# Seven block products in half of one output projection: forgetting attention in a two-block transformer kernel on one Trainium2 core

## What is computed

```python
h = x @ w_in                      # q, k, v, forget logits, gate: 4 x 1024 + 16 columns
cum = jnp.cumsum(log_sigmoid(f_logit + b_f), axis=1)
o = _dense_causal(q, k, v, 64 ** -0.5, cum)          # 16 heads of 64
y = (o * jax.nn.silu(gate)) @ w_out                  # w_out: 1024 x 1024
x = _layernorm(8 ** 0.25 * x + y, ln_g, ln_b)
```

## Time and profile before

| | |
|---|---|
| median of three runs | 1783.54 us (1783.27 to 1784.11) |
| the profiled execution | 1783.37 us |
| its span, first to last instruction | 1781.6 us |
| PE busy | 1762.7 us, 99% of the span |
| DVE, ACT, POOL busy | 992.2, 811.2, 727.9 us |
| share of PE in the chain that ended last | 89% |
| mean granted TensorE clock | 0.998 of full |

### The profile page before, as it was taken

How to read it: one execution, slowest core, us unless ns; L and a number is a source line. 1 busy time by engine, 2 the same in 40 slices (tenths; PEclk the granted TensorE clock), 3 DMA queues, 4 the chain that set the end, 5 groups by cost and what they waited for, 6 DMA issues and landing times.

```text
span 1781.6 us, 24874 instructions
## 1 busy us (share of the span) xinstructions
PE 1762.7 (99%) x9776; PEld 1416.7 (80%) x9776; DVE 992.2 (56%) x2091; ACT 811.2 (46%) x1737; POOL 727.9 (41%) x441
## 2 busy tenths in 40 slices
PE   9999999999999999999999999999999999999997
PEld 6787877788888888889776798888877777887676
DVE  4558688564351524254777368755644352567764
ACT  5434455453342323244467345554345343446662
POOL 4534521154686868643322333234332324332122
PEclk9999999999999999999999999999999999999999
DMA  5322320153505151333212232123331322331211
GB/s 173 100 71 72 95 60 25 36 174 93 170 25 177 36 165 48 95 90 93 60 36 83 83 99 72 60 71 94 97 92 50 79 63 90 99 68 38 63 52 72
DMA packets 215032, 147.94 MB, mean 83 GB/s; under 512 B 51825, under 2 KB 197249, under 8 KB 214914
## 3 DMA queue, kind: packets, MB, share of 16 engines
q1 hardware_dynamic: 210592, 137.10, 26.6%
q10 hardware_dynamic: 4322, 9.24, 1.6%
HBM read 144.22 MB, written 2.10 MB: 82 GB/s over the span
## 4 chain that ended last, share of the span: by engine, by line
PE 89%; DVE 7%; ACT 3%; issue 1%; DMA 0%; POOL 0%; SPq 0%; DVEq 0%; ACTq 0%
PE PS L427 24%; PE PS L429 23%; PE PS L428 23%; PE PS L515 6%; PE PS L577 6%; PE PS L601 4%; PE PS L779 1%; DVE PS L1645 1%; ACT X L1172 1%; DVE X L1648 1%; DVE PS L1664 1%; PE PS L1033 1%; PE PS L802 1%; PE PS L1054 0%; DVE P L2188 0%
## 5 line engine op out<-in xcount | busy, mean ns | idle before, releaser
L2291 POOL TENSOR_TENSOR Wl<-Wr,Wh 128x1024 fp32r<-128x1024 f32 (+3 forms) x367 | 601.6, 1660 | 1001.9 <-ACT Wh L1113 1001.6
L427 PE MATMUL PS<-XTl,Wh 128*128 128x512 f32 (+1 forms) x1096 | 412.9, 377 | 1.0 <-DVE KF L1683 0.8
L429 PE MATMUL PS<-XTh,Wh 128*128 128x512 f32 (+1 forms) x1096 | 408.1, 372 | 0.0
L428 PE MATMUL PS<-XTh,Wl 128*128 128x512 f32 (+1 forms) x1096 | 408.0, 372 | 0.0
L1113 ACT CAST Wh<-Wr 128x1024 fp32r<-128x1024 f32 (+5 forms) x274 | 249.3, 931 | 154.5 <-PE PS L429 96.1
L427 PEld LDWEIGHTS PS<-XTl,Wh 128*128 128x128 f32 x1096 | 206.5, 188 | 45.6 <-issue 9.9
L429 PEld LDWEIGHTS PS<-XTh,Wh 128*128 128x128 f32 x1096 | 206.4, 188 | 36.5
L428 PEld LDWEIGHTS PS<-XTh,Wl 128*128 128x128 f32 x1096 | 206.6, 188 | 34.7
L427 PE MATMUL PS<-Wl,XTh 128*128 128x512 f32 (+2 forms) x608 | 227.3, 374 | 1.7 <-DVE XTl L1656 1.2
L429 PE MATMUL PS<-Wh,XTh 128*128 128x512 f32 (+2 forms) x608 | 224.1, 369 | 0.0
L428 PE MATMUL PS<-Wh,XTl 128*128 128x512 f32 (+2 forms) x608 | 224.0, 368 | 0.0
(11 more groups left out here) (342 smaller groups left out, 2748.7 us busy)
## 6 DMA issues: line engine op xcount, KB each, us to landing
Wr<-in_w_in SPq DMA_DIRECT2D x38, 512.0 KB, 3.6
Wr<-in_fox_w_in SPq DMA_DIRECT2D x32, 512.0 KB, 4.2
Wr<-in_w_ffn_gate SPq DMA_DIRECT2D x22, 512.0 KB, 3.9
Wr<-in_w_ffn_up SPq DMA_DIRECT2D x22, 512.0 KB, 3.9
Wr<-in_swa_w_in SPq DMA_DIRECT2D x20, 512.0 KB, 3.8
WP<-in_w_ffn_down SPq DMA_DIRECT2D x9, 1024.0 KB, 9.2
Wr<-in_mla_w_in SPq DMA_DIRECT2D x16, 512.0 KB, 4.1
Wr<-in_mla_w_out SPq DMA_DIRECT2D x16, 512.0 KB, 3.2
```

What stands on the lines that cost most here:

```text
L427: pe.matmul(o, l[0], r[1], start=start, stop=False, skip_group_check=again)
L428: pe.matmul(o, l[1], r[0], start=False, stop=False, skip_group_check=again)
L429: return pe.matmul(o, l[0], r[0], start=False, stop=stop, skip_group_check=again)
L2291: ins = raw.tensor_tensor(l[:, cs], r[:, cs], h[:, cs].bitcast(F), sub)
```

## The change

In `fox`, the contraction tiles a = 0..3 of the output projection are computed by Winograd's form of the product of 2x2 blocks, with seven block products instead of eight; a = 4..7 stay as they were. Tile pairs (0,1) and (2,3) are q = 0 and q = 1. For each q the left factor becomes seven 256-token factors, the weights four raw pieces: the even row with its right half replaced by a sum ("even"), two sums of halves ("sums"), the odd row as it is ("odd"), and one more sum ("fours", of which both q share one piece). Gate 3 and gate 5 get a new step `factors` on ACT and DVE; `gated` is left out for f = 0..3; POOL gets `sums7`; the odd rows are loaded twice, once for the sums and once as a piece. PE runs `outproj7`; DVE folds four partial results per token half into `X` (`combine`) before the residual. The due number at the last gate projection (`g7`) is one higher. PE's part and the pieces:

```diff
+SEVENS = {'fox': (3, 5)}
...
+            if c in SEVENS and kind in ("sums", "fours"):
+                return O7[c][1 if kind == "sums" else 2][:, :, :].rearrange("p a n -> p (a n)")
...
+        def released(entry):
+            if entry in odd_of:
+                return by_pool.at("fours", *homes[odd_of[entry]][1:])
+            return weight_lo.at(entry)
...
+        def overlaid(s, q):
+            if s == "fox":
+                return [scores_full.at(s, 3 + 3 * q, 1, 3)]
...
-                    due[signal, key] = min(count[0] + AHEAD + (key[:2] == ("swa", 1)) + 2 * (key == ("fu", 21)), len(used) + W_SLOTS)
+                    due[signal, key] = min(count[0] + AHEAD + (key[:2] == ("swa", 1)) + 2 * (key == ("fu", 21)) + (key == ("g", "fox", 7)), len(used) + W_SLOTS)
...
+            def outproj7(s, src, lhs, ready, turned=True):
+                A, B, C, E = ([take(("y", s, v + i, c)) for v in range(2)] for i, c in ((0, 0), (2, 1), (0, 1), (2, 0)))
...
+                def product(bs, v, w, h, j, q, start, stop, again=False):
+                    e.wait_ge(weight_lo.at(w), *free(bs[v]), by_dve.at("fs", s, q))
+                    return mm3(PS[bs[v]][:, :], [t[:, q, j, tile(v)] for t in FS], part(w, 0, D, 512 * h, 512 * h + 512), start, stop, again)
+                for q in range(2):
+                    w2 = weight(row(2 * q), D, ("even", s, q))
+                    odd_src[w2] = row(2 * q + 1)
+                    w13 = weight(row(2 * q), D, ("sums", s, q))
+                    for bs, w, h, j, x in ((A, w2, 0, 0, "A"), (B, w2, 1, 5, "B"), (C, w13, 0, 4, "C"), (E, w13, 1, 3, "E")):
+                        for v in range(2):
+                            ins = product(bs, v, w, h, j, q, q == 0, q == 1)
...
+                for q in range(2):
+                    wo = weight(row(2 * q + 1), D, ("odd", s, q))
+                    if q == 0:
+                        w4 = weight(row(0), D, ("fours", s, 0))
+                    for bs, w, h, j, x in ((A, wo, 0, 1, "A"), (C, wo, 1, 6, "C"), (E, w4, q, 2, "E")):
+                        for v in range(2):
+                            e.wait_ge(by_dve.at("part", s, x, v))
+                            ins = product(bs, v, w, h, j, q, False, False, again=True)
...
+                ws = [(weight(row(a), D), a) for a in range(4, 8)]
+                for i in range(NT):
+                    for c in range(2):
+                        b, fresh = place[i, c], i >= 2 and c == 1
```

ScalarE's part of `factors`, and the call in its list of steps:

```diff
+            def factors(s, q):
+                g = GT[s][:, 2 * q:2 * q + 2, :].rearrange("p f (a t) -> p (f a) t", a=2)
+                e.wait_ge(by_dve.at(s, "o", 2 * q + 1), *overlaid(s, q))
+                high(FS[0][:, q, 0, :], g[:, 0, :], "fs_hi", s, q)
+                high(FS[0][:, q, 1:3, :], g[:, 2:4, :], "fs_hi", s, q)
+                e.wait_ge(by_dve.at("sf", s, q))
+                high(FS[0][:, q, 3:7, :], S4[:, :, :], "fs_hi", s, q)
...
-                elif kind == "out":
+                elif kind == "gate" and x in SEVENS.get(s, ()):
+                    factors(s, SEVENS[s].index(x))
+                elif kind == "out" and (x >= 4 or s not in SEVENS):
                     gated(s, x)
```

VectorE's `combine` and its part of `factors`:

```diff
+            def combine(s):
+                for x in "ACEB":
+                    for v in range(2):
...
+                        e.wait_ge(psum_full.at("part", s, x, v), by_dve.now())
+                        if x in "AB":
+                            scale = ALPHA if x == "A" else 1.0
+                            ve.scalar_tensor_tensor(low, low, scale, b, mult, add).then_inc(*by_dve.next())
+                            ve.scalar_tensor_tensor(right, right, scale, b.unsqueeze(1).broadcast_to([128, 2, 512]), mult, sub).then_inc(*by_dve.next("part", s, x, v))
+                        else:
+                            y = X[:, v + 2, HALVES[1]]
+                            ve.tensor_tensor(y, y, b, add if x == "C" else sub).then_inc(*by_dve.next("part", s, x, v))
...
+            def factors(s, q):
+                ve.tensor_tensor(S4[:, 0, :], g[:, 0, :], g[:, 1, :], sub).then_inc(*by_dve.next())
+                ve.tensor_tensor(S4[:, 1, :], g[:, 1, :], g[:, 3, :], sub).then_inc(*by_dve.next())
+                e.wait_ge(by_dve.now())
+                ve.tensor_tensor(S4[:, 2, :], S4[:, 1, :], g[:, 0, :], sub).then_inc(*by_dve.next())
+                e.wait_ge(by_dve.now())
+                ve.tensor_tensor(S4[:, 3, :], S4[:, 2, :], g[:, 2, :], add).then_inc(*by_dve.next("sf", s, q))
+                e.wait_ge(by_act.at("fs_hi", s, q), by_dve.now())
+                low(FS[1][:, q, 0, :], g[:, 0, :], FS[0][:, q, 0, :], "fs", s, q)
+                low(FS[1][:, q, 1:3, :], g[:, 2:4, :], FS[0][:, q, 1:3, :], "fs", s, q)
+                low(FS[1][:, q, 3:7, :], S4[:, :, :], FS[0][:, q, 3:7, :], "fs", s, q)
```

GpSimd's sums, called before the rest of the piece "even" of q, and SyncE's loop:

```diff
+            def sums7(i, s, q):
+                e.wait_ge(raw_in[slots[0]].at(i), raw_in[slots[1]].at("odd", i), *([weight_lo.at(at_home["sums", s, 0])] if q else [by_dve.at("fs", s, 1)] if s == "swa" else []))
+                raw.tensor_tensor(t[:, 0, :], w[:, HALVES[0]], w[:, HALVES[1]], add).then_inc(*by_pool.next())
+                raw.tensor_tensor(t[:, 1, :], w[:, HALVES[1]], o[:, HALVES[1]], add).then_inc(*by_pool.next("sums", s, q))
+                e.wait_ge(by_pool.now())
+                raw.tensor_tensor(w[:, HALVES[1]], t[:, 0, :], o[:, HALVES[1]], add).then_inc(*by_pool.next("even", s, q))
+                e.wait_ge(by_pool.now())
+                raw.tensor_tensor(f[:, q, :], w[:, HALVES[1]], o[:, HALVES[0]], add).then_inc(*by_pool.next("fours", s, q))
...
+                for key, srcs in ((i, srcs), (("odd", i), odd_src.get(i))):
...
+                    if ring[key] >= RAW_SLOTS:
+                        e.wait_ge(released(ringed[ring[key] - RAW_SLOTS]))
```

More of the change, by code:

```diff
@@ L560, in outproj, with row @@
                     if norm and turned and i in (1, 2):
+                        turn_tile(s, i - 1)
+                used[ws[-1][0]] = psum_full.at("y", s, NT - 1, 1)
+            def outproj7(s, src, lhs, ready, turned=True):
+                A, B, C, E = ([take(("y", s, v + i, c)) for v in range(2)] for i, c in ((0, 0), (2, 1), (0, 1), (2, 0)))
+                place = {(v + i, c): bs[v] for bs, i, c in ((A, 0, 0), (B, 2, 1), (C, 0, 1), (E, 2, 0)) for v in range(2)}
+                FS = O7[s][0]
+                def row(a):
+                    return [(src[:, a:a + 1, :], 0)]
+                def product(bs, v, w, h, j, q, start, stop, again=False):
[8 more added lines that the diff above has]
+                            ins = product(bs, v, w, h, j, q, q == 0, q == 1)
+                            if q:
+                                ins.then_inc(*done(psum_full, "part", s, x, v))
+                        if h:
+                            if not q:
+                                ins.then_inc(*weight_used.next())
+                            used[w] = psum_full.now() if q else weight_used.now()
+                for q in range(2):
[6 more added lines that the diff above has]
+                            ins = product(bs, v, w, h, j, q, False, False, again=True)
+                        if h:
+                            ins.then_inc(*weight_used.next())
+                            used[w] = weight_used.now()
+                ws = [(weight(row(a), D), a) for a in range(4, 8)]
+                for i in range(NT):
+                    for c in range(2):
+                        b, fresh = place[i, c], i >= 2 and c == 1
+                        if fresh:
+                            e.wait_ge(by_dve.at("part", s, "B", i - 2))
+                        for w, a in ws:
+                            e.wait_ge(weight_lo.at(w), *ready(a))
+                            ins = mm3(PS[b][:, :], pair(lhs, ALL, a, tile(i)), part(w, 0, D, 512 * c, 512 * c + 512), fresh and a == 4, a == 7, again=not fresh)
+                            if i == NT - 1 and c == 1 and a < 7:
+                                ins.then_inc(*weight_used.next())
+                                used[w] = weight_used.now()
+                        ins.then_inc(*done(psum_full, "y", s, i, c))
+                        give(b, (by_dve, ("normed", s, i, c)))
+                    if turned and i in (1, 2):
@@ L1091, in tensor @@
                     give(b, (by_dve, (s, "o", x)))
-            outproj(s, by_rows(A["fox_w_out_2"][0]), XT, lambda a: [by_dve.at("fox", "out", a)])
+            outproj7(s, by_rows(A["fox_w_out_2"][0]), XT, lambda a: [by_dve.at("fox", "out", a)])
             mla(1)
@@ L2119, in mla @@
                         gate_values(s, x)
-                    elif kind == "out":
+                        if x in SEVENS.get(s, ()):
+                            factors(s, SEVENS[s].index(x))
+                    elif kind == "out" and (x >= 4 or s not in SEVENS):
                         gated(s, x)
```

70 lines of the change are left out of this document (53 added, 17 removed).

## The result

The changed kernel takes 1788.08 us (median of 12 executions, 1785.72 to 1790.33) against 1783.77 us (12, 1782.65 to 1784.22) of the kernel before: 1.0024 times as long, 95% interval 1.0015 to 1.0032. The forecast was 1785.8 in a range that ended at 1787.6.

What follows compares the result with a forecast made beforehand. PE was taken to bound the kernel, busy 1762.7 of 1781.6 us. It would lose 2.72 us of matmuls but wait for late pieces, reaching a = 7 2.3 us later: 1783.54 + 2.3 = 1785.8, range 1783.0 to 1787.6.

Steps and rivals of the forecast that it cites:

- Slower clock: Rival, 13%: PE stands twice around 1508 to 1512, the granted clock falls to its lower level, adding 1.8 us; 1787.6.
- The copies: DVE's `PT` copies of pair 6 wait behind the second half's factors at gate 5 and come 5.0 us late.
- The scaling: ACT's scaling of pair 7, behind the late DVE work, goes from 1469.69 to 1474.7, 5.0 us late.
- The tanh: ACT's tanh of g7, behind rounding of POOL's late sums, starts at 1485.9 instead of 1483.63, 2.3 us late.
- Gate 7: On DVE, behind rests of f = 4 to 6 beside POOL's, gate 7 starts at 1491.7, 2.6 us late.
- POOL's row: POOL's seven weight-piece rests in a row begin 3.77 us after gate 7, at 1495.45 instead of 1492.85.
- The first half's factors: The factors made at gate 3 cost nothing: 5 us on DVE inside 8.42 idle us.
- Turns: DVE's and POOL's rests alternate an instruction at a time near gate 7; without turns, a 15% rival, 1783.4.
- PE's 2.72 us: In the projection's half a = 0..3, PE does 84 matmuls instead of 96, which takes 2.72 us from it.
- The sum: PE gets to a = 7 of part (0,0) at 1512.05 instead of 1509.76, so the kernel is 2.3 us slower.
- PE's stands on the way: PE waits about 1.7 us at the first round's last bank, 1.5 at a = 6 and 1.7 at a = 7.
- Where the 2.72 went: The account of the saved PE time as lost in three PE waits: last bank, a = 6 and a = 7.

Runs made afterwards that it cites:

- e1: The changed kernel run again with no edit, for its spread and a second profile: 1788.11 us, 1.0025 times the kernel before.
- e4: The changed kernel with six useless matmuls ahead of a = 6 and six ahead of a = 7 in part (0,0): 1785.40 us.
- e5: The changed kernel without the higher due number for the last gate, so ACT rounds three pieces ahead of it and not four: 1789.25 us.
- e6: The changed kernel with POOL's two rests that run beside DVE's rests 4 to 6 cut into four instructions each: 1785.84 us.
- e9: The changed kernel with second-half factors at gate 4, ACT rounding one piece ahead of them, and the second round reordered to free the "fours" slot earlier: 1781.59 us.
- e2: The changed kernel with the second half's factors at gate 4 instead of gate 5: 1784.07 us, 1.0006 times the kernel before.
- e3: The changed kernel with gate 7 ahead of DVE's rests of f = 4 to 6 in `fox`: 1784.93 us, 1.0009 times the kernel before.

## Why the prediction was wrong

The step that failed is a term of the sum: it put the clock behind PE's stands at nothing. The prediction had the schedule, its stands and the price of the clock, "Slower clock, 1787.6 (+4.1)", and gave that rival 13% against 64% for the same schedule at full clock. The runs turn it round: nine of the change's twelve executions have the lower mean clock, and all seven of e1; with the stands filled (e4) none has. The rival's price was about right: 1.8 forecast from the program's first matmuls, 1.80 measured between the two stages, 1.6 of it by the clock. What spoke for it was in the trace and was read as nothing: "there is no row of so broken a stretch at full speed" was a reason not to expect full speed. Nor was the stand of 1.33 at 1099.30 read. It has the full clock behind it in the trace before and the lower level in e5 and e6, so that row alone would have misled. The range ended exactly on the rival's value, 1787.6, and left its own scatter out; the median lies 0.48 above. Of this 0.23 belongs to the kernel before, which had 1783.77 beside the change and not 1783.54.

Point by point for the rest:

- The copies 5.0 us late: 4.99. The scaling 5.0: 5.00. The tanh 2.3: 2.39. Gate 7 2.6: 2.58. POOL's row 2.6 (1492.85 to 1495.45): 2.58. The first half's factors and `combine`: no wait of PE on either in the change's projection; before the first residual DVE still sits idle for 8.05.
- Turns: right for the rests, as e6 shows. f = 4 to 6 were to be done 4.6 us after 1487.15; the three took 4.50.
- PE's 2.72 us: right. The 84 matmuls of the sevens run from 1486.04 to 1504.98 in e9, 18.94 us from the first start to the last, and the first 84 before take the same (1485.83 to 1504.77). What e9 lacks of the 2.72 is the 0.32 at a = 7.
- The sum: a = 7 of part (0,0) starts 2.27 later than before, and +2.29 was reckoned (1512.05 for 1509.76). This is the chain through POOL's row, step by step, and no luck. PE's stands on the way were less exact. They were to be 1.7, 1.5 and 1.7, counted by PE's starts; by its starts they are 1.17 (1490.35 to 1491.74, less the usual 0.23), 1.49 and 1.54. The brackets in the timeline (1.00, 1.33, 1.37) are shorter, since they begin when the matmul ahead has ended. And PE came to the projection 0.50 late, put at "a few tenths". Neither moves a = 7, which waits for POOL.
- A stand costs more than its bracket: from the first to the last of the 84 matmuls the change takes 1485.69 to 1505.96, 1.33 us longer than e9, with a bracket of 1.00 in it.
- "Where the 2.72 went" left out a bound: even with the row in time, a = 7 waits for the slot of "fours" (1.59 in e2 and e3). It did not show in the change, but undoing the late factors alone would not have brought the gain.

Open: what decides, behind the same stands, whether the clock falls in an execution.

## What to carry to other kernels

A change that leaves PE less work and another engine no less turns a full PE into one that stands now and then; price each such stand twice, by its wait and by the clock behind it, and where no row shows the engine standing like this at full clock, give the slower case at least an even chance. When an edit's gain is eaten by waits, look for the next wait in line too: taking away the late factors alone (e2) brought the seven products back to the old time, and only with the slot of "fours" freed as well did they pay. Put side work on an engine into the stretch where it idles, and check which instruction of a neighbour it will have to take turns with.

## What the runs showed of the chip that was not expected

- Behind stands of 1.01, 1.30 and 1.56 us the clock was at its lower level for most of four windows of 1 us (0.53, 0.50, 0.50, 0.77 in e1); behind 1.00, 1.33 and 1.37 in the same program it stayed at 1.00 (the change's first profile). A single stand of 1.32 at about 1100 us was followed by the lower level in two profiles (e5, e6) and by the full clock in eight.
- Twelve useless matmuls made the kernel 2.7 us faster (e4 against e1), 1.74 of it in the stage.
- Cutting POOL's rests in four cost POOL 1.79 us beside DVE (3.28 and 3.73 us for 2.38 and 2.84) and gave DVE 1.37 us in three instructions; the stage became 1.27 shorter (296.50 against 297.77).
